# VectorE's sums of gathered rows in the late expert pairs, placed behind the gating step and the copy of the down product

## The reference, cut to what matters

```python
def expert_block(args):
    xb, gb = args
    h = jax.nn.silu(jnp.einsum('td,edf->tef', xb, w_gate)) * jnp.einsum('td,edf->tef', xb, w_up)
    h = h * gb[..., None].astype(h.dtype)
    return jnp.einsum('tef,efd->td', h, w_down)
...
shared = (jax.nn.silu(xf @ p['ws_gate']) * (xf @ p['ws_up'])) @ p['ws_down']
return (routed + shared).astype(x.dtype).reshape(B, T, D)
```

## Time and profile before

| | us |
|---|---|
| median of 3 runs (1073.39 to 1075.11) | 1073.66 |
| the profiled execution | 1079.33 |
| its span, first to last instruction | 1077.5 |
| PE busy | 940.6 |
| DVE busy | 530.1 |
| POOL busy | 361.8 |
| ACT busy | 233.8 |
| sums of gathered rows (line 1045), 48 | 61.5 |
| gathers for them (line 1167), 48 | 50.3 |
| copies of down products (line 981), 32 | 22.1 |

### The profile page before, as it was taken

One profiled execution on the slowest core, in us unless ns is written; L12 is line 12 of the kernel. 1 busy time (PEld: TensorE's weight loads), 2 busy tenths in 40 slices (PEclk: granted clock), 3 DMA queues, 4 the chain that ended last, 5 costly groups with the idle time before them and its releaser, 6 DMA issues. The chain is left out here.

```text
span 1077.5 us, 17882 instructions
## 1 busy us (share of the span) xinstructions
PE 940.6 (87%) x7285; PEld 565.1 (52%) x7285; DVE 530.1 (49%) x1034; ACT 233.8 (22%) x486; POOL 361.8 (34%) x393
## 2 busy tenths in 40 slices
PE   5999999999999977799988989878897879878795
PEld 4878877877887776367433334333332333333231
DVE  2158958866885869854233121120112353423585
ACT  3241134115213411541111111111111111111013
POOL 0049908943990696001111010111104132311330
PEclk9999999999999999899999899988998989888898
DMA  8645253425523274296899999999999999999931
GB/s 229 172 125 199 80 163 126 167 81 168 187 101 119 71 266 165 101 420 250 338 419 420 421 417 415 409 407 419 406 414 411 398 382 399 402 418 361 397 91 42
DMA packets 90924, 295.67 MB, mean 274 GB/s; under 512 B 19746, under 2 KB 51044, under 8 KB 65991
## 3 DMA queue, kind: packets, MB, share of 16 engines
q1 hardware_dynamic: 72647, 254.03, 61.6%
q0 software_dynamic: 18192, 40.46, 10.0%
HBM read 284.13 MB, written 36.30 MB: 297 GB/s over the span
## 5 line engine op out<-in xcount | busy, mean ns | idle before, releaser
L1355 PE MATMUL bank<-big 64*64 64x64 f32 (+5 forms) x6818 | 880.9, 360 | 115.4 <-DMA big<-in_w_up 67.4
L1355 PEld LDWEIGHTS bank<-big 64*64 64x64 f32 (+2 forms) x6818 | 511.9, 150 | 435.3 <-issue 348.7
L1652 ACT ACTIVATE big<-bank 128x512 f32<-128x512 f32 (+7 forms) x286 | 122.8, 453 | 680.3 <-PE bank L1355 386.6
L1152 POOL DMA_INDIRECT big<-xg,big x32 | 34.1, 1064 | 455.4 <-PE bank L587 379.2
L2146 POOL TENSOR_SCALAR big<-big 128x256 f32<-128x256 f32 x120 | 132.6, 1105 | 1.7
L972 DVE TENSOR_TENSOR big<-big,bank 128x256 f32<-128x256 f32 x32 | 13.5, 421 | 234.5 <-ACT big L1652 234.5
L2158 POOL TENSOR_TENSOR big<-big 128x256 f32<-128x256 f32 x120 | 94.4, 787 | 0.3
L1942 DVE SCALAR_TENSOR_TENSOR big<-big 128x256 f32<-128x256 f32 x120 | 79.9, 665 | 4.1
L1045 DVE SCALAR_TENSOR_TENSOR big<-big 128x1024 f32<-128x1024 f32 (+1 forms) x48 | 61.5, 1281 | 23.4 <-DMA big<-yrows,big 20.6
L1167 POOL DMA_INDIRECT big<-yrows,big x48 | 50.3, 1047 | 50.7 <-DVE big L1045 27.0
L1652 ACT ACTIVATE big<-big 128x272 f32<-128x272 f32 (+9 forms) x108 | 49.8, 505 | 43.2 <-DVE big L1877 11.3
(11 more groups left out here) (166 smaller groups left out, 415.4 us busy)
## 6 DMA issues: line engine op xcount, KB each, us to landing
big<-in_w_gate SPq DMA_DIRECT2D x64, 1024.0 KB, 17.2
big<-in_w_up SPq DMA_DIRECT2D x64, 1024.0 KB, 22.9
big<-in_w_down SPq DMA_DIRECT2D x64, 1024.0 KB, 15.1
big<-in_w_in SPq DMA_DIRECT2D x29, 1024.0 KB, 5.4
yrows<-big POOLq DMA_DIRECT2D x32, 512.0 KB, 3.4
big<-in_w_out SPq DMA_DIRECT2D x2, 2048.0 KB, 16.8
big<-in_state_wkv SPq DMA_DIRECT2D x32, 64.0 KB, 2.2
out_wkv_s<-big SPq DMA_DIRECT2D x32, 64.0 KB, 4.0
```

Of the source, the lines that this page charges most:

```text
L1152: pool.indirect_dma_start(out=x[0:n, :], out_offset=None, in_=xg, in_offset=bass.IndirectOffsetOnAxis(ap=idxu[0:n, col:col + 1], axis=0), ...
L1355: return nc.tensor.matmul(out_, lhsT=lhsT, rhs=rhs, start=start, stop=stop)
L1652: return nc.scalar.activation(out_, in_, f, **kw)
```

## The change

In pairs 28, 29 and 30 the call of add_early moves from behind add_late(q - 2) to the end of the pair, behind hidden(q) and take(q - 1). In pair 31 it stays where it was. The shares of rows, the buffers, the gathers and all other engines' programs are the same.

```diff
@@ -989,14 +989,16 @@
                     late_gates(q + NLATE)
                 if q >= FIRST + 2:
                     add_late(q - 2)
+                if q == NPAIR - 1:
                     add_early(LATE_ROWS[q - FIRST - 2], LATE_ROWS[q - FIRST - 1])
-                if q == NPAIR - 1:
                     take(q - 1)
                 if DOWN_AT <= q < DOWN_AT + NDOWN - 1:
                     shared_rows(q - DOWN_AT)
                 hidden(q)
                 if 0 < q < NPAIR - 1:
                     take(q - 1)
+                if FIRST + 2 <= q < NPAIR - 1:
+                    add_early(LATE_ROWS[q - FIRST - 2], LATE_ROWS[q - FIRST - 1])
                 if q == DOWN_AT + NDOWN - 1:
                     shared_rows(NDOWN - 1)
                 if HALF + 3 <= q < HALF + 11:
```

## The result

The changed kernel takes 1086.52 us (median of 4 runs, 1086.24 to 1088.15) against 1073.53 us (4 runs): a ratio of 1.0121, 95% interval 1.0104 to 1.0139, so **13.0 us slower**. The forecast was 1088.1, 14.4 us slower.

A forecast was written before the change was run, and what follows sets the result against it. From about 995 us the hand-over of work between TensorE and VectorE was taken as the bound, not the weight stream. Delays of 12.5 + 1.9 = 14.4 us on the median 1073.66 gave 1088.1 us, range 1082.0 to 1093.5.

The forecast's parts named there:

- No room behind the copy: Pairs 28 to 30: moved sums precede add_late, for which TensorE's fourth combine product waits; gaps 8.8 and 7.5 us.
- Pair 29, +1.6: TensorE's fourth combine product in pair 29 starts 1.6 us later, behind three moved sums; the clock stays up.
- combine(28) 3.9 earlier: In pair 30 TensorE's combine starts 3.9 us earlier, at 1014.8 instead of 1018.71; the stall for the copy is gone.
- Fourth product of pair 30, +3.5: Pair 30's fourth combine product comes 3.5 us later, waiting for seven sums, row 33's gather and two add_late sums.
- The clock in pair 30, +1.9: Slow TensorE products behind the gap ahead of pair 30's fourth combine product add 1.9 us.
- Pair 31, +7.1 and +1.9: Pair 31's fourth combine product waits for seven sums and two of add_late, +7.1 us; slow clock behind it, +1.9.
- The end moves with it: Behind pair 31's fourth product the chain is as before, so the kernel's end moves by 14.4 us.
- (a): Rival: the clock stays up and the late gathers cost nothing, 1082.6 us; chance 0.05.
- (b): Rival: late gathers, 8.6 us for rows 33 and 40, 1096 us at the most, 1092 with half the surplus; chance 0.07.
- (c): Rival: faster, sums find room behind take and combine(28) starts earlier without slow clock, -5.8 us, 1067.9 us; chance 0.04.
- (d): Rival: TensorE gains 5.8 us in pair 30, loses about that in pair 31, within 2 us of 1073.7; chance 0.04.

The follow-up runs named there:

- e1: Only pair 28's block of sums moved behind the copy, pairs 29 and 30 in the order of before; ratio 0.9998 to the kernel before.
- e3: Only pair 30's block of seven sums moved behind the copy, the rest in the order of before; ratio 1.0097 to the kernel before.
- e2: Only pair 29's block of seven sums moved behind the copy, the rest in the order of before; ratio 1.0023 to the kernel before.
- e4: Changed kernel with combine's fourth and fifth products in banks 6 and 7, the down product waiting for add_late; ratio 0.9995 to the kernel before.
- e6: Changed kernel with the sums of rows 24 to 47 cut to 64 of 1024 columns; ratio 1.0021 to the kernel before.

## Why the prediction was right

- **No room behind the copy.** Right. TensorE's waits show line 1030 in place of 981, and the gaps stand where they were forecast, 8.31 and 6.81 against 8.8 and 7.5.
- **Pair 29, +1.6.** The fourth product started 993.47 - 989.61 = 3.86 after combine(27), before it was 998.19 - 995.73 = 2.46 (998.14 and 0.05 from the earlier trace rows): +1.4. The gap of 1.32 left the clock up, as assumed (5.57 behind it); the assumption was less safe than it looked, since the kernel before has a fall behind a gap of 1.52 (last section). The delay is swallowed when it is alone (e1).
- **combine(28) 3.9 earlier.** 1008.46 - 989.61 = 18.85 against 22.98: 4.1 earlier.
- **Fourth product of pair 30, +3.5.** 29.70 after combine(27) against 26.80: +2.9. The gather's latency was taken as 6.5, the middle between 4.4 and 8.6 and no reading of a row; both ends were of 128-row gathers, and that the middle came near is in part luck. GpSimd issued row 33 at 1010.93 and VectorE began with it at 1016.93, so 6.0; and each of the chained steps was a little shorter.

```profile
1009.32 1.31 POOL L1169 DMA_INDIRECT big<-yrows,big  x1 [13.49 <-DVE big L1047]
1010.93 1.07 POOL L1169 DMA_INDIRECT big<-yrows,big  x1 [0.30 <-issue]
```

  The estimate by the Trainium skill ("DMA: Bandwidth & Descriptors", "Anatomy of one DMA — SWDGE (gpsimd) path"), 2.1 us and no wait, does not hold while the weights stream: rows 32 to 36 took 6.0 to 7.0 from issue to landing. Row 39, also of eight rows, issued at 1036.67 with one last transfer of weights (1 MB) in flight, took 2.4, near that estimate.
- **The clock in pair 30, +1.9: the mis-sized term.** The group behind the gap took 7.13, 1.6 more than the 5.57 at the full clock. But the working set it against nothing, and before, the same stretch was not at its shortest either: from the fourth product at 1022.53 to the transposes at 1028.56 it took 6.0, since the fifth product waited for VectorE's third sum, which came late behind a slow third product and ended at 1023.86. So the net is 1.0. At the transposes of pair 30 the changed kernel is 3.9 late (1026.37 - 989.61 against 1028.56 - 995.73), not 5.4. VectorE before:

```profile
1023.17 0.69 DVE L1028 TENSOR_TENSOR big<-big,bank 128x512 f32<-128x512 f32 x1 [0.69 <-PE bank L1355]
```

- **Pair 31, +7.1 and +1.9.** From there 6.9 more to the fourth product, 10.8 in all (55.59 against 44.76) for 12.5 forecast, and 2.2 for the clock. Rows 39 and 40 were in time. e3 has this block by itself, +9.3 in the late part for 9.0. What a slow clock adds to the group of 20 is no constant: 1.6 and 2.2 here, 1.9 in e2, 2.8 in e3 (7.13, 7.78, 7.49 and 8.35 against 5.57), so the prediction's 1.9 for each was right only to within about 1 us. Its "near 1045.5" for the end of combine(29)'s third product does not follow from its own numbers (1038.04 + 5.4 + 2.5 = 1045.9), but enters no sum.
- **The end moves with it.** Right: VectorE idles 1.48 ahead of the last gating step, against 1.06.

The sum is 2.9 + 1.0 + 6.9 + 2.2 = 13.0 for 3.5 + 1.9 + 7.1 + 1.9 = 14.4: the path and the waits as forecast, three terms too large by 0.6, 0.9 and 0.2, the last too small by 0.3. Of the rivals, (a) falls by the clock's 0.50, (b) by the 6.0 for row 33 and the missing waits for rows 39 and 40, (c) and (d) by the result; that (c) would have decided at the wait of line 671 is what e4 shows, though with this wait gone the order is only as good as before, since its cost goes to the down product and the copy.

## What to carry to other kernels

Before moving work behind a hand-over, read what is next on the same engine: a block is free only in front of something that nobody waits for yet, and a bank that is used twice in a row makes the producer wait for a consumer queued behind that block. When a block of work is late because its data is late, move the transfer in its own queue, not the block in its engine's. And do the sum for each iteration by itself: here blocks of 3, 7 and 7 sums in three neighbouring pairs cost 0, 3 and 9 us.

## What was not expected of the hardware

TensorE ran a stretch faster for having been given more to do: 16 more instructions into each of two gaps of 7 to 8 us kept the granted clock at 1.00, and the kernel became 3.4 (profile) to 4.6 us (ratios) faster than the changed one. The length of a gap alone does not settle whether the clock falls: behind the 3.08 of e6 it stayed at 1.00 (5.57 for the group of 20), while behind 1.52 in the kernel before it fell to 0.51 (5.35 for 16 instructions that took 3.65 at 1059.14, at the full clock):

```profile
609.62 5.35 PE L1355 MATMUL bank<-big 128*64 128x512 f32 x16 [1.52 <-DMA big<-in_w_up]
...
1059.14 3.65 PE L1355 MATMUL bank<-big 128*64 128x512 f32 x16 [0.47 <-ACT big L1652]
```

An eight-row gather (32 KB) from HBM took 6.0 to 7.0 us from issue to landing while all queues together moved 377 GB/s, and 2.4 with one last weight transfer in flight. The 128-row gather of row 47 in the kernel before took at most 4.4 from issue to use, late in the kernel. In the profiled execution of before VectorE idled 3.47 us in pair 28, and TensorE 3.11 with it:

```profile
974.87 0.16 DVE L943 TENSOR_SCALAR big<-bank 128x1 uint32<-128x1 f32 x1 [3.47 <-remote]
```

In the changed kernel TensorE idled 0.61 at this place, and so it did in each experiment's profile. What the 3.47 us were stays open. With the slow clock behind them they make 3.11 - 0.61 + 10.87 - 8.03 = 5.3 us, about what that execution was over the median.
